# A two-layer SSM, attention and mixture-of-experts trunk: the layer loop written out, small loads moved to another queue, and v projected in two halves between scan steps

## The chip, the cores and the metric

The kernel runs on one core of one Trainium2 chip. The metric is the device time of one execution in microseconds (us), lower being better. A core has a matrix engine (TensorE, PE in the rows, with its weight loads as PEld), a vector engine (VectorE, DVE), an activation engine (ScalarE, ACT), a general engine (GpSimd, POOL) and a sync engine (SyncE, SP) that issues most of the transfers here. Each engine runs its own instructions in the order in which they are written; they meet through semaphores.

## What is computed

Everything is float32, with one sequence of 256 tokens of width 1024 and two layers. The reference, cut to what matters:

```python
for l in range(DEPTH):                                   # DEPTH = 2
    h = rms_norm(x, norm1_g[l])
    u, q, k, v, g_ssm, g_attn = jnp.split(h @ w_in[l], splits, axis=-1)
    y_ssm = s5_branch(u, a_re, a_im, log_dt, b_re, b_im, c_re, c_im, d_skip, w_glu)
    q = apply_rope(rms_norm(q, q_norm_g[l]), cos, sin)   # 8 heads of 64
    k = apply_rope(rms_norm(k, k_norm_g[l]), cos, sin)
    y_attn = moba_attention(q, k, v) @ w_attn[l]         # causal, 256 tokens
    x = x + (sigmoid(g_ssm) * y_ssm + sigmoid(g_attn) * y_attn) @ w_out[l]
    h2 = rms_norm(x, norm2_g[l])
    x = x + hier_moe(h2, ...)                            # 32 experts, 2 chosen per token

# s5_branch: dt = exp(log_dt); abar = exp((lam_re + i lam_im) dt); B scaled by f(abar, lam)
#   state[t] = abar * state[t-1] + B u[t];  y = Re(C state) + d * u;  z = gelu(y)
#   return (z @ w_glu)[:1024] * sigmoid((z @ w_glu)[1024:])
```

## The kernel before

Each of the five engines has one instruction stream, written out by hand, inside a hardware loop over the two layers (`Fori(0, DEPTH)`). A layer has a **front** (projections, state-space scan, attention, output projection, routing) and an **expert phase** of 11 units. A unit holds three experts (the last one two), and all 32 experts' weights are streamed through.

**Weights.** The tile `pool_all` is 11 slots of 2 MB (128 partitions by 4096 floats). SP issues every weight load, each when a semaphore says that the slot is free. In the front, slots 0 and 1 hold first the columns of u and q, then the gate columns of the state-space branch, then `w_glu`; slots 2 and 3 hold the columns of k and v, then the attention gates. `front_used` counts the uses that have ended. The same slots feed the expert units. Scratch of the front lives in the other slots.

**Small loads.** ACT's queue carries the rows for the gains and the poles (`rows`), the step sizes (`log_dt`), and B and C of the state-space model (`b_raw`, `c_raw`). Those of the first layer are issued at the start of the program. Those of the second layer are issued at the start of the first layer's expert phase. SP's queue carries the head gains (`qk_gain`) and the router's weights, behind the loads of slots 0 to 3.

**Order of the front.** PE: `project_u` (L586), `spread_rms` (L595), the three projections `project_qkv` of q, k and v (L610), `setup_matrices` (the transposes L555 and L562 of B and C), `scan_input` 0 and 1 (L628). Then come six steps of `gate(k)`, `scan_output(k)`, `scan_input(k + 2)` (L725, L643, L628), and then attention, mixed with gates 6 and 7, the last two `scan_output` and the GLU projection `ssm_project` (L757). DVE: `setup_first` (a serial chain of 128x16 and 128x32 operations, L1266 to L1351), the scaling of u, `angles` (L1249 to L1261), the head norms, `rope_k` for both halves (L1487 to L1494), `c_lhs` (L1542), and eight times `scan(k)` (L1416 to L1430) with `skip` (L1440) between. ACT: the sines, `heads_out` (L1064, L1068), the scaled copies of v (L1119), `b_lhs` (L1123), then `gate_tanh` (L1100) and `gelu` (L1077) in turn. POOL: `setup` (L1870 to L1882), the router's scaling (L1895), the rope tables (L1898, L1901), `rope_q` (L1961 to L1968), and eight times `rotate(k)` (L1918) with `gelu(k - 1)` (L1940 to L1950).

A scan step goes PE `scan_input`, DVE `scan`, POOL `rotate`, PE `scan_output`, DVE `skip`, POOL and ACT `gelu`. `setup_first` waits for the semaphore `setup_in`, which counts `log_dt` and all of B and C.

## Time and profile before

| | |
|---|---|
| median of 3 runs | 1474.98 us (1473.22 to 1476.66) |
| profiled execution, its own time | 1474.61 us |
| its span, first to last instruction | 1472.8 us |
| busy: PE, DVE, POOL, ACT | 1188.9, 434.6, 187.0, 159.7 us |
| moved by DMA | 462.28 MB, 314 GB/s over the span |

A timeline row gives the start in us, the duration, the engine (SPq and ACTq are transfers issued from those queues), the line in the kernel, the operation, output and input, and how many instructions were merged. Brackets at the end give how long the engine had been idle and what released it. "issue" there means that nothing in the profile was waited for. PE's float32 matmuls appear as two records each. The chain of waits runs back from the last instruction and shows at each step what was late.

### The profile page before, as it was taken

How to read it: one execution, taken by the hardware profiler on the slowest of the kernel's cores; microseconds unless marked ns; L12 is line 12 of the kernel's file. 1: busy time of each engine (PE TensorE's matmuls, PEld its weight loads, DVE VectorE, ACT ScalarE, POOL GpSimd, SP SyncE). 2: the span in 40 equal slices, each digit the busy share in tenths (PEclk: the TensorE clock that was granted, in tenths of full speed). 3: DMA queues.
4: the chain of work that ended last, by engine and by line, in shares of the span. 5: the costliest groups of instructions: out<-in, count | busy, mean ns of one | idle time of the engine just before them, and what ended most of it. 6: DMA issues, size and time to landing. Idle time of an engine off the chain costs nothing.

```text
span 1472.8 us, 19284 instructions
## 1 busy us (share of the span) xinstructions
PE 1188.9 (81%) x7371; PEld 541.1 (37%) x7372; DVE 434.6 (30%) x874; ACT 159.7 (11%) x313; POOL 187.0 (13%) x250
## 2 busy tenths in 40 slices
PE   7959799779777677777889888997778776778787
PEld 5334454524322233222254445444333232223232
DVE  1888622322101011101157894223111110011111
ACT  1230220300000000000013103112000000000000
POOL 0558600000000000000015574000000000000000
PEclk9969899899989899988999998998999988888889
DMA  9322067379999999999942220971999999999995
GB/s 296 136 93 115 1 254 321 123 329 428 428 429 428 429 429 429 429 428 428 422 165 114 115 115 16 383 285 51 427 428 429 428 429 429 429 428 428 429 429 227
DMA packets 57934, 462.28 MB, mean 314 GB/s; under 512 B 19964, under 2 KB 20120, under 8 KB 32280
## 3 DMA queue, kind: packets, MB, share of 16 engines
q1 hardware_dynamic: 46624, 460.39, 74.9%
q10 hardware_dynamic: 11256, 1.17, 0.7%
q8 instruction: 34, 0.56, 0.2%
q14 instruction: 20, 0.16, 0.0%
HBM read 460.49 MB, written 1.05 MB: 313 GB/s over the span
## 4 chain that ended last, share of the span: by engine, by line
DMA 40%; PE 36%; issue 7%; DVE 7%; POOL 6%; ACT 2%; SPq 1%; ACTq 1%; POOLq 0%; DVEq 0%
DMA pool_all<-in_w_gate_up_dram 39%; PE ps L912 15%; PE ps L757 4%; PE ps L781 4%; POOL pool_all L1918 3%; PE ps L929 2%; PE ps L725 2%; PE ps L739 2%; PE ps L873 2%; DVE pool_all L1430 1%; PE ps L586 1%; SPq L441 1%; PE ps L896 1%; PE ps L698 1%; ACTq L1016 1%
## 5 line engine op out<-in xcount | busy, mean ns | idle before, releaser
L912 PE MATMUL ps<-pool_all 128*32 128x512 f32 (+1 forms) x2816 | 368.8, 684 | 150.2 <-DMA pool_all<-in_w_gate_up_dram 150.2
L912 PEld LDWEIGHTS ps<-pool_all 128*32 128x32 f32 x2816 | 97.4, 124 | 416.7 <-issue 411.1
L929 PE MATMUL ps<-pool_all 128*32 128x512 f32 (+1 forms) x1408 | 160.6, 609 | 25.2 <-DMA pool_all<-in_w_down_dram 19.6
L1663 DVE SCALAR_TENSOR_TENSOR pool_all<-pool_all,ps 128x512 f32<-128x512 f32 x22 | 15.1, 688 | 547.6 <-ACT pool_all L1197 547.6
L725 PE MATMUL ps<-pool_all,hT 128*128 128x512 f32 x256 | 118.5, 617 | 0.0
L873 PE MATMUL ps<-pool_all,hT 128*128 128x128 f32 x704 | 92.1, 294 | 15.4 <-issue 10.7
L873 PEld LDWEIGHTS ps<-pool_all,hT 128*128 128x128 f32 x704 | 87.9, 207 | 32.4 <-issue 27.4
L929 PEld LDWEIGHTS ps<-pool_all 128*32 128x32 f32 x1408 | 45.9, 112 | 124.8 <-issue 124.7
L1197 ACT ACTIVATE pool_all<-ps 128x512 f32<-128x512 f32 x22 | 13.1, 597 | 688.7 <-PE ps L912 688.7
L1918 POOL TENSOR_TENSOR pool_all<-pool_all 128x512 f32<-128x512 f32 x64 | 79.7, 1279 | 40.0 <-DVE pool_all L1430 40.0
L610 PE MATMUL ps<-pool_all,hT 128*128 128x512 f32 x192 | 82.7, 592 | 0.0
L896 PE MATMUL ps<-pool_all 128*128 128x512 f32 x176 | 81.4, 605 | 0.0
L1870 POOL TENSOR_TENSOR pool_all<-pool_all,cst 128x512 f32<-128x512 f32 x4 | 4.2, 1065 | 575.0 <-DVE vec L1287 539.6
L725 PEld LDWEIGHTS ps<-pool_all,hT 128*128 128x128 f32 x256 | 49.2, 198 | 58.4 <-issue 57.3
L1676 DVE COPY pool_all<-ps 128x512 f32<-128x512 f32 x22 | 15.2, 692 | 177.3 <-PE ps L929 177.3
L757 PE MATMUL ps<-pool_all 128*128 128x512 f32 x128 | 56.5, 594 | 0.0
L781 PE MATMUL ps<-pool_all,hT 128*128 128x512 f32 x128 | 56.4, 594 | 0.0
L610 PEld LDWEIGHTS ps<-pool_all,hT 128*128 128x128 f32 x192 | 36.3, 190 | 45.0 <-issue 45.0
L896 PEld LDWEIGHTS ps<-pool_all 128*128 128x128 f32 x176 | 31.6, 189 | 50.0 <-issue 50.0
L643 PE MATMUL ps<-pool_all 128*32 128x128 f32 x512 | 19.9, 303 | 29.9 <-POOL pool_all L1918 29.8
L1653 DVE TENSOR_TENSOR pool_all<-ps,gain 128x512 f32<-128x512 f32 x44 | 30.0, 682 | 43.8 <-PE ps L873 43.8
L1416 DVE TENSOR_TENSOR pool_all<-ps,pool_all 128x512 f32<-128x512 f32 x64 | 39.6, 678 | 1.9 <-PE ps L628 1.7
(252 smaller groups left out, 982.5 us busy)
## 6 DMA issues: line engine op xcount, KB each, us to landing
pool_all<-in_w_gate_up_dram SPq DMA_DIRECT2D x128, 2048.0 KB, 25.4
pool_all<-in_w_down_dram SPq DMA_DIRECT2D x64, 2048.0 KB, 27.1
pool_all<-in_w_in_dram SPq DMA_DIRECT2D x16, 2048.0 KB, 12.6
pool_all<-in_w_glu_dram SPq DMA_DIRECT2D x4, 2048.0 KB, 11.0
pool_all<-in_w_out_dram SPq DMA_DIRECT2D x4, 2048.0 KB, 20.0
pool_all<-in_w_attn_dram SPq DMA_DIRECT2D x2, 2048.0 KB, 7.4
xs<-in_x_dram SPq DMA_DIRECT2D x1, 1024.0 KB, 5.1
out_dram<-xs SPq DMA_DIRECT2D x2, 512.0 KB, 2.8
```

What stands on the lines that cost most here:

```text
L610: mm = pe.matmul(ps[:, bank + t], hT[:, k, t * P:(t + 1) * P], wide_slot(slot + k // 4)[:, k % 4, col:col + 512], start=(k == 0), stop=(k ...
L725: mm = pe.matmul(ps[:, GATE_BANK[j]], hT[:, k, t * P:(t + 1) * P], wide_slot(slot + k // 4)[:, k % 4, 512 * half:512 * half + 512], start= ...
L739: mm = pe.matmul(ps[:, u % 2], oT[:, c, t * P:(t + 1) * P], wide_slot(2)[:, c, 512 * half:512 * half + 512], start=(c == 0), stop=(c == 3))
L757: mm = pe.matmul(ps[:, GLU_BANK[u] + w], uT[:, k, t * P:(t + 1) * P], slot_cols(k // 2).rearrange("p (k c n) -> p k c n", k=2, c=2)[:, k % ...
L781: mm = pe.matmul(ps[:, WO_BANK[t] + half], hT[:, k, t * P:(t + 1) * P], wide_slot(9 + k // 4)[:, k % 4, 512 * half:512 * half + 512], star ...
L873: mm = pe.matmul(ps[:, 2 + k // 4, (k % 4) * P:(k % 4 + 1) * P], x_rows[:, t, k], pick[:, t], start=(t == 0), stop=(t == NT - 1))
L896: mm = pe.matmul(ps[:, 4 + 2 * t + half], backT[:, t], ybuf[:, half], start=first, stop=False, skip_group_check=True)
L912: mm = pe.matmul(ps[r, half], xT[:, k, r], lane_cols(n, TRIO * h, k % 4, half), start=(k == 0), stop=(k == KC - 1), skip_group_check=True)
L929: mm = pe.matmul(ps[r, 2 + half], ffT[:, c, r], lane_cols(n, 2 * TRIO, c, half), start=(c == 0), stop=(c == 3), skip_group_check=True)
L1416: ve.tensor_tensor(out4[o], x, table, ALU.mult).then_inc(dve_layer, 1)
L1653: ve.tensor_tensor(xT[:, 4 * h:4 * h + 4], ps[:, 2 + h].rearrange("p (k s) -> p k s", k=4), wide(gain2[:, 4 * h:4 * h + 4], 2, [4, P]), AL ...
L1918: pool.tensor_tensor(post[:, v], wst[:, r], table[:, tiles, 0:HALF], ALU.mult).then_inc(rotated, 1)
```

## The change

1. **The layer loop is written out** on all five engines: `for l in range(DEPTH)` in Python. The hardware branches at the layer boundary are gone, and so are the last layer's preparations for a layer that doesn't exist. The loops over expert units stay.
2. **Small loads.** `log_dt` joins the rows on ACT's queue, and its semaphore is now `rows_in`. B, C and the head gains go on SP's queue, between slots 0 and 1 and slots 2 and 3, under `setup_in`. DVE's `setup_first` waits for `rows_in` alone.
3. **v** is no longer projected before the scan. `project_v(0)` and `project_v(1)`, one 128-token tile each, take the places of `gate(0)` and `gate(1)` in the steps, and every gate moves two steps down. The steps are eight now, and attention begins after the eighth.
4. **DVE's `rope_k`** moves from ahead of the scan to between `skip(6)` and `skip(7)`.
5. **POOL's scaling of the router's weights** moves from ahead of the rope tables to the end of its layer.

The diff, cut to its core:

```diff
-        with sp.Fori(0, DEPTH) as l:
+        for l in range(DEPTH):
...
             load_rows(0, win_d, 0, U0)
             load_rows(1, win_d, 4, U0)
-            sp.wait_ge(unit_used, at(unit_used, l, -1))
+            for r, b in enumerate((ssm_b_re, ssm_b_im)):
+                load_setup(b_raw[:, r], b[one_layer].rearrange("o (i g) s h -> (o g s) i h", g=2))
+            for r, c in enumerate((ssm_c_re, ssm_c_im)):
+                load_setup(c_raw[:, r], c[one_layer].rearrange("o (q g) h s -> (o g h) q s", q=QUADS))
+            for w, g in enumerate((q_norm_g, k_norm_g)):
+                load_setup(qk_gain[:, w], g[one_layer].to_broadcast([P, HD]))
+            if l:
+                sp.wait_ge(unit_used, at(unit_used, l, -1))
             load_rows(2, win_d, 0, V0)
...
+            def project_v(t):
+
+                pe.wait_ge(b_ready, at(b_ready, l, 4))
+                for k in range(KC):
+                    mm = pe.matmul(ps[:, t], hT[:, k, t * P:(t + 1) * P], wide_slot(2 + k // 4)[:, k % 4, 512:1024],
+                                   start=(k == 0), stop=(k == KC - 1))
+                mm.then_inc(front_used if t else v_mm, 1)
...
-            project_qkv("q")
-            project_qkv("k")
-            project_qkv("v")
+            project_qk("q")
+            project_qk("k")
             setup_matrices(l)
             scan_input(0)
             scan_input(1)
-            for k in range(6):
-                gate(k)
+            for k in range(8):
+                if k < NT:
+                    project_v(k)
+                else:
+                    gate(k - NT)
                 scan_output(k)
-                scan_input(k + 2)
+                if k < 6:
+                    scan_input(k + 2)
             turn_heads(0)
-            scan_output(6)
+            gate(6)
             turn_heads(1)
             scores(0)
-            gate(6)
+            gate(7)
             turn_probs(0)
             scores(1)
-            scan_output(7)
             values(0)
-            gate(7)
+            ssm_project(0)
             turn_probs(1)
...
-            ve.wait_ge(setup_in, at(setup_in, n, per[setup_in.name]))
+            ve.wait_ge(rows_in, at(rows_in, n, per[rows_in.name]))
...
             skip(6)
+            rope_k(0)
+            rope_k(1)
+            skip(7)
             softmax_in(0)
-            skip(7)
             attention_out(0)
```

How instructions stand now. PE after the projections of q and k, before: three groups L610 (q, k, v), the two groups of transposes, `scan_input` 0 and 1 (L628), `gate(0)` (L725).

```order
L595 MATMUL ps<-pool_all,cst 128x128 x2
L610 MATMUL ps<-pool_all,hT 128x512 x16
L576 ISA
L610 MATMUL ps<-pool_all,hT 128x512 x16
L603 REGISTER_ALU
L610 MATMUL ps<-pool_all,hT 128x512 x16
L550 ISA
L552 REGISTER_ALU
L555 MATMUL ps<-cst,pool_all 128x128 x8
L562 MATMUL ps<-cst,pool_all 128x128 x8
L628 MATMUL ps<-pool_all 128x128 x16
```

The same place after: L616 is q and k together, L624 is a half of v, L640 is `scan_input`, L655 is `scan_output`.

```order
L604 MATMUL ps<-pool_all,cst 128x128 x2
L616 MATMUL ps<-pool_all,hT 128x512 x32
L564 MATMUL ps<-cst,pool_all 128x128 x8
L571 MATMUL ps<-cst,pool_all 128x128 x8
L640 MATMUL ps<-pool_all 128x128 x16
L624 MATMUL ps<-pool_all,hT 128x512 x8
L655 MATMUL ps<-pool_all 32x128 x16
L640 MATMUL ps<-pool_all 128x128 x8
L624 MATMUL ps<-pool_all,hT 128x512 x8
```

The 16 matmuls of v have left the stretch ahead of the first scan step and stand as two groups of 8 in the first two steps.

PE at the end of the scan, before: `gate(5)`, `scan_output(5)`, `scan_input(7)`, the turn of q (L658), `scan_output(6)`, the turn of k, `scores(0)` (L680), `gate(6)`.

```order
L725 MATMUL ps<-pool_all,hT 128x512 x8
L640 REGISTER_ALU
L643 MATMUL ps<-pool_all 32x128 x16
L628 MATMUL ps<-pool_all 128x128 x8
L658 MATMUL ps<-cst,pool_all 128x128 x8
L640 REGISTER_ALU
L643 MATMUL ps<-pool_all 32x128 x16
L658 MATMUL ps<-cst,pool_all 128x128 x8
L680 MATMUL ps<-pool_all 128x128 x8
L725 MATMUL ps<-pool_all,hT 128x512 x8
```

After, from `gate(4)` (L737) on; L670 is a turn and L692 is `scores(0)`.

```order
L737 MATMUL ps<-pool_all,hT 128x512 x8
L655 MATMUL ps<-pool_all 32x128 x16
L737 MATMUL ps<-pool_all,hT 128x512 x8
L655 MATMUL ps<-pool_all 32x128 x16
L670 MATMUL ps<-cst,pool_all 128x128 x8
L737 MATMUL ps<-pool_all,hT 128x512 x8
L670 MATMUL ps<-cst,pool_all 128x128 x8
L692 MATMUL ps<-pool_all 128x128 x8
L737 MATMUL ps<-pool_all,hT 128x512 x8
```

Both turns and `scores(0)` now stand behind the last `scan_output`.

SP at the start of a layer, after (before, the two small loads of the head gains stood behind all four loads of `w_in`, and B and C were not on this queue):

```order
L431 DMA pool_all<-in_w_in_dram 128x4x1024 x2
L444 DMA pool_all<-in_ssm_b_re_dram 128x16x16
L444 DMA pool_all<-in_ssm_b_im_dram 128x16x16
L444 DMA pool_all<-in_ssm_c_re_dram 128x4x64
L444 DMA pool_all<-in_ssm_c_im_dram 128x4x64
L444 DMA qk_gain<-in_q_norm_g_dram 128x64
L444 DMA qk_gain<-in_k_norm_g_dram 128x64
L431 DMA pool_all<-in_w_in_dram 128x4x1024 x2
L438 DMA router_w<-in_router_w_group_dram 128x8x4
```

The weights of k and v (the second L431) now stand behind six small loads.

## Rows read from the trace of the kernel before

**Rows 1.** The chain that ended last, by line, from the page.

```profile
DMA pool_all<-in_w_gate_up_dram 39%; PE ps L912 15%; PE ps L757 4%; PE ps L781 4%; POOL pool_all L1918 3%; PE ps L929 2%; PE ps L725 2%; PE ps L739 2%; PE ps L873 2%; DVE pool_all L1430 1%; PE ps L586 1%; SPq L441 1%; PE ps L896 1%; PE ps L698 1%; ACTq L1016 1%
```

**Rows 2.** Timeline, first layer: DVE's setup chain, first angle, ACT's first head output.

```profile
35.58 0.18 DVE L1266 TENSOR_SCALAR pool_all<-log_dt 128x32 f32<-128x32 f32 x1 [22.03 <-DMA pool_all<-in_ssm_c_im_dram]
...
50.41 1.67 DVE L1249 TENSOR_TENSOR pool_all<-cst,turns_hi 128x1032 f32<-128x1032 f32 x1
...
72.65 1.25 ACT L1064 ACTIVATE pool_all<-ps,rstd 128x512 f32<-128x512 f32 x2
```

**Rows 3.** Timeline, first layer, PE: project_u, and q with k and v behind it.

```profile
12.54 15.83 PE L586 MATMUL ps<-hT,pool_all 128*128 128x256 f32 x64 [0.88 <-DMA pool_all<-in_w_in_dram]
...
28.65 31.92 PE L610 MATMUL ps<-pool_all,hT 128*128 128x512 f32 x74
```

**Rows 4.** First layer: last rows load, PE's turn; log_dt's two loads, to landing.

```profile
2.48 0.55 ACTq L1005 DMA_DIRECT2D rows<-in_ssm_a_im_dram  x1
...
7.74 0.32 PE L545 MATMUL ps<-cst,rows 52*128 52x52 f32 x1 [7.74 <-DMA rows<-in_ssm_a_im_dram]
...
DMA to landing us min/median/max: 3.1/5.3/7.4
```

**Rows 5.** B's first load for layer two; a window (columns: busy, PEclk, DMA, GB/s).

```profile
288.51 0.40 ACTq L1016 DMA_DIRECT2D pool_all<-in_ssm_b_re_dram  x1
...
296.00:300.00 4.00, 4.00 (x42) 1.17 (x36) 2.82 (x15) 0.00 (x0) 0.00 (x0) 1.00 0.00 0
```

**Rows 6.** Timeline, first layer, from the head norms to the first scan steps.

```profile
80.48 1.25 ACT L1119 ACTIVATE pool_all<-ps,rstd 128x512 f32<-128x512 f32 x2
...
80.99 0.69 DVE L1487 TENSOR_TENSOR pool_all<-pool_all,head_ss 128x512 f32<-128x512 f32 x1
...
84.18 3.77 PE L628 MATMUL ps<-pool_all 64*128 64x128 f32 x32 [3.12 <-ACT pool_all L1123]
...
93.24 2.48 DVE L1416 TENSOR_TENSOR pool_all<-ps,pool_all 128x512 f32<-128x512 f32 x4
...
95.63 0.68 DVE L1419 TENSOR_TENSOR pool_all<-pool_all 128x512 f32<-128x512 f32 x1
...
99.66 5.03 POOL L1918 TENSOR_TENSOR pool_all<-pool_all 128x512 f32<-128x512 f32 x4 [10.33 <-DVE pool_all L1430]
...
102.09 1.56 DVE L1419 TENSOR_TENSOR pool_all<-pool_all 128x512 f32<-128x512 f32 x1
```

**Rows 7.** Timeline at the layers' boundary and in the second layer's front.

```profile
752.75 16.07 PE L586 MATMUL ps<-hT,pool_all 128*128 128x256 f32 x64 [5.47 <-issue]
...
754.96 0.08 DVE L1378 MEMSET ov_slot<- 128x28 f32 x1 [4.22 <-issue]
...
766.99 0.17 DVE L1351 TENSOR_TENSOR f_im<-f_im,den 128x16 f32<-128x16 f32 x1
...
770.90 1.77 DVE L1249 TENSOR_TENSOR pool_all<-cst,turns_hi 128x1032 f32<-128x1032 f32 x1
...
792.13 1.25 ACT L1064 ACTIVATE pool_all<-ps,rstd 128x512 f32<-128x512 f32 x2
...
822.25 5.03 POOL L1918 TENSOR_TENSOR pool_all<-pool_all 128x512 f32<-128x512 f32 x4 [13.88 <-DVE pool_all L1430]
```

**Rows 8.** Timeline, first layer, from the end of the scan to ssm_project(2).

```profile
158.77 1.06 PE L658 MATMUL ps<-cst,pool_all 128*128 128x128 f32 x8 [0.69 <-ACT pool_all L1100]
...
169.57 4.58 POOL L1918 TENSOR_TENSOR pool_all<-pool_all 128x512 f32<-128x512 f32 x4 [1.11 <-DVE pool_all L1430]
...
171.74 2.08 PE L680 MATMUL ps<-pool_all 64*128 64x128 f32 x16 [1.25 <-ACT pool_all L1134]
...
173.75 8.51 PE L725 MATMUL ps<-pool_all,hT 128*128 128x512 f32 x16
...
186.97 7.09 PE L725 MATMUL ps<-pool_all,hT 128*128 128x512 f32 x16
...
216.68 7.03 PE L757 MATMUL ps<-pool_all 128*128 128x512 f32 x16
```

More of the change, by code:

```diff
@@ L571, in _ @@
         norm(0)
-        with pe.Fori(0, DEPTH) as l:
+        for l in range(DEPTH):
             def weights(i, turn):
@@ L834, in _ @@
             values(1)
-            ssm_project(0)
+            ssm_project(1)
             turn_probs(2)
             values(2)
-            ssm_project(1)
             turn_attention()
@@ L919, in unit @@
                     pe.wait_ge(main["xT"], at(main["xT"], l, 2 * i + 4))
-                if last:
+                if last and l < DEPTH - 1:
                     setup_vectors(l + 1)
@@ L994, in _ @@
             unit(UNITS - 1, 2, duo_lanes, last=True)
-            pe.nop()
-            with pe.If(l < DEPTH - 1):
+            if l < DEPTH - 1:
                 norm(l + 1)
-            pe.nop()
     @block.scalar
@@ L1047, in _ @@
         norm_squares(0)
-        load_setup(0)
-        with act.Fori(0, DEPTH) as l:
+        for l in range(DEPTH):
             act.dma_start(gain2, norm2_g[bass.ds(l, 1)].rearrange("o (p k) -> (o p) k", k=KC)).then_inc(gain_in, 16)
@@ L1116, in _ @@
             heads_std(1)
-            act.wait_ge(front_used, at(front_used, l, 2))
-            for t in range(NT):
-                act.activation(vtok[:, t], ps[:, 6 + t], ACT.Copy, scale=rstd[:, t:t + 1]).then_inc(v_raw, 1)
             act.wait_ge(bt_mm, at(bt_mm, l, 1))
@@ L1124, in _ @@
                                    scale=const("odd_tile")[:, o:o + 1]).then_inc(b_ready, 1)
-            for k in range(6):
-                gate_tanh(k)
+            for k in range(8):
+                if k < NT:
+                    if k == 0:
+                        act.wait_ge(v_mm, at(v_mm, l, 1))
+                    else:
+                        act.wait_ge(front_used, at(front_used, l, 2))
+                    act.activation(vtok[:, k], ps[:, k], ACT.Copy, scale=rstd[:, k:k + 1]).then_inc(v_raw, 1)
+                else:
+                    gate_tanh(k - NT)
                 gelu(k)
@@ L1131, in _ @@
                 act.copy(qT[:, 2 * n:2 * n + 2].rearrange("p c s -> p (c s)"), ps[:, n]).then_inc(qT_ready, 1)
+            gate_tanh(6)
             act.wait_ge(qk_turned, at(qk_turned, l, 2))
@@ L1135, in _ @@
             exps(0)
-            gelu(6)
-            gate_tanh(6)
+            gate_tanh(7)
             probs_turned(0)
             exps(1)
-            gelu(7)
-            gate_tanh(7)
+            glu_sigmoid(0)
             probs_turned(1)
             exps(2)
-            glu_sigmoid(0)
+            glu_sigmoid(1)
             probs_turned(2)
-            glu_sigmoid(1)
             act.wait_ge(o_turned, at(o_turned, l, 1))
@@ L1373, in _ @@
         norm_scale(0)
-        with ve.Fori(0, DEPTH) as l:
+        for l in range(DEPTH):
             L = counted(dve_layer, l)
```

71 lines of the change are left out of this document (26 added, 45 removed).

## The prediction

> **What bounds the kernel now.** I read the chain of waits first. 39% of the span in it is the experts' gate and up weights arriving, and the lines of PE, DVE and POOL that follow belong to the two fronts [rows 1]. So the kernel alternates: from the second expert unit of each layer on it runs at the pace of its weight stream, which this change leaves alone in bytes and order, and before that a front runs in which compute engines hand work to each other. Every load of the first expert units is tied to a step of the front, so a front that ends earlier by some time moves the expert phase by the same time. The question is what the change does to each front.
>
> Then I read the timeline of the first front for what is late. Three stretches matter.
>
> Stretch one is up to the first head output. DVE sits idle 22.03 us until 35.58, waiting for C's last load, and only then starts its serial chain. The angles start at 50.41 and ACT's first head output, T below, at 72.65, which is 22.2 us after the angles [rows 2]. PE is far ahead: `project_u` runs from 12.54 to 28.4 and q, k and v follow without a gap, at 74 records in 31.92 us, so 13.8 us for each projection of 32 records [rows 3].
>
> Stretch two is from T to the first `rotate`. It holds ACT's copies of v (80.48), DVE's `rope_k` from 80.99, PE's `scan_input` at 84.18, DVE's first scan at 93.24 and POOL's first `rotate` at 99.66, before which POOL was idle 10.33 us [rows 6]. DVE decides it, as PE's operands for the scan were there 9 us before DVE came.
>
> Stretch three is the scan and what follows. From the first `rotate` at 99.66 to the last, which ends at 174.15, POOL and DVE set the pace, and from `scores(0)` at 171.74 PE has hardly an idle moment up to `ssm_project(2)` at 216.68 [rows 6, 8].
>
> In the second layer DVE doesn't wait for loads. There PE idles 5.47 us and DVE 4.22 us for nothing that the profile shows, exactly at the branch that closes the layer loop. u runs from 752.75 to 768.8, the angles start at 770.90, T is 792.13 and the first `rotate` is at 822.25 [rows 7].
>
> **Stretch one, first layer.** DVE now waits for the rows and `log_dt` only. Its chain then lies beside `project_u`: in the second layer it takes 12.2 us from the first memset to its last product (754.96 to 767.16) [rows 7]. Started at about 14.5 it ends near 27, ahead of u. The next to be late is PE's u. In the second layer the angles start 2.1 us after u ends (768.8 to 770.90) [rows 7], so with u's end at 28.4 they would start at 30.5. One cost comes in: PE's turn of the rows waits for all loads under `rows_in`, now with `log_dt`, and PE's 3.9 us of work between the turn (7.74) and its readiness for u (12.54 less the 0.88 of waiting) stands behind it. ACT issues `log_dt` after the last rows load, so from 3.0, and its two loads took 3.1 and 7.4 us to land [rows 3, 4]. Landing at 6.1 costs nothing, landing at 10.4 makes u start at 14.3, 1.8 us late. I take 1.3, near the loaded case. The angles then start at 31.8, 18.6 us earlier than 50.41, and T is 54.0. The projection of k ends near 57.5 (u's end 29.7, two times 13.8, and the small spread between them), and ACT needs it 3.9 us after T, so it just fits.
>
> B, C and the head gains now travel ahead of the weights of k. Alone, the B and C loads had all landed within 7.5 us of the first issue (288.51 to 296.00) [rows 5]. Before, all that was issued at the start had landed by 35.6 [rows 2], the bytes are the same, and PE needs the k columns at 43.7 (u's end and one projection). So this costs 0, and if it is late, each us late is a us of k. POOL's setup hides behind q and k.
>
> **Stretch one, second layer.** Without the branch PE goes on from the turn of x at 747.3, so u ends by about 763. DVE's memsets follow its norm at 750.8 instead of 754.96, so its chain ends at 763.0, a little later than u, and the angles start at 764.6, which is 6.3 us earlier. T is 785.8. If the gap stays, the gain here is 0.
>
> **Stretch two.** `rope_k` and the v copies have gone. From T, ACT's b operands took until PE's 84.18, which is 11.5 us, and lose the 1.1 us of the two v copies: 10.4. DVE's scan starts when the first of the two scan inputs is in, for which I take 1.6, a little under half of their 3.77 us, at T + 12.0, since its own `c_lhs` is done by then. The scan took 6.4 us (93.24 to 99.6). But it now runs beside POOL's `rope_q`, which ended at 99.66 less 10.33, so at 89.33 or T + 16.7. The DVE addition L1419 took 0.68 us with POOL idle and 1.56 us beside `rotate` [rows 6], and the scan has two such operations there, so I add 1.9 (0 to 2.6). The first `rotate` starts at T + 20.3. First layer: 54.0 + 20.3 = 74.3 against 99.66, a gain of **25.3**. Second layer: 785.8 + 20.3 = 806.1 against 822.25, a gain of **16.1**.
>
> The Trainium skill (SBUF — State Buffer, section "SBUF: two separate sides") says that a DVE operation with two SBUF inputs and a GpSimd operation take one pair of ports by an exclusive lock, and that the other blocks wholly. It speaks against moving the scan beside `rope_q`, and the two L1419 rows agree with it; without it this stretch would be 1.9 us shorter in each layer.
>
> **Stretch three.** The eight scan steps keep their order on DVE and POOL. v's halves are as long as the gates they replace. Steps seven and eight now hold `gate(4)` and `gate(5)` where PE was half idle. What is paid is the attention: two turns and `scores(0)` stood in those idle times and now stand behind the last `scan_output`. Counted from the end of the last `rotate`, against before:
> - ACT frees the banks for the turn only after `gelu(6)` and `gate_tanh(5)`: +2.5, in which `scan_output(7)` hides, -1.1
> - two turns at 1.06: +2.1; k's copy to SBUF between turn and scores, as ACT's pair of v copies (1.25): +1.2
> - `scores(0)`: 2.08 at the low clock, about half at the high one: +1.6
> - `gate(6)` was 8.51 us on a PE that had idled, `gate(7)` 7.09: -1.4; it had begun 0.4 before the `rotate` ended: +0.4
> - the last `rotate` beside `rope_k` instead of an idle DVE, 5.03 against 4.58 us: +0.45
> - `turn_attention` follows `values(2)` at once and waits for DVE: +0.9
>
> That is **6.7 us** lost in each layer [rows 6, 8]. The bounds are 4 (the turns find idle PE time after all) and 10 (`rope_k`, which filled most of 80.99 to 93.24 before the scan, holds up `skip(7)` and with it ACT, whose copies of q stand behind `gelu(7)`). What follows `ssm_project(2)` is in the same order.
>
> **Sum.** First layer 25.3 - 6.7 = 18.6. Second layer 16.1 - 6.7 = 9.4. The last layer's dropped turn of rows is 0.3. Together 28.3 us off the profiled execution's 1474.61: 1446.3. The median of the runs shown is 0.4 above that execution, so I predict **1446.7**.
>
> **Rivals.**
> 1. *The boundary gap stays.* For it: the profile names no releaser, and expert loops are left just before, with a branch of their own. Against it: both gaps sit at the loop's end. Then the second layer's 6.3 is lost: 1453.0. Chance 0.12. The Trainium skill (Runtime: NRT & Kernel Launch, section "Instruction fetch mechanics") says that a taken branch out of the prefetched window stalls the engine for a fetch, and recommends unrolling. By it the gap goes, and I lean that way.
> 2. *The small loads hold the weights of k.* PE found slot 1 landed in the middle of u, at 20.5. If B and C then take the 22 us that DVE waited for them beside the weights [rows 2], and the 4.2 MB behind them 13.4 at the mean 314 GB/s of the table, slots 2 and 3 land at 55.9 instead of by 43.7, and the first layer pays 12.2: 1458.9. Chance 0.06.
> 3. *Slower.* The same mechanism in both layers, with the k columns late by more than 28 us in all: the head gain is eaten and the 6.7 of stretch three remains twice. With both head gains gone it gives 1474.98 + 13.4 = 1488.4. It decides from slots 2 and 3 landing some 19 us late in the first layer and 10 in the second. The 7.5 us of rows 5 speak against it. Chance 0.04.
> 4. *The costs are smaller.* `log_dt` lands early (1.3), no contention (3.8), and waits on constants instead of registers save a little: 1441. Chance 0.12.
> 5. The forecast, 1443 to 1451 with its own bounds: 0.66.
>
> **Range.** Low: the cheap case with the tail's lower bound, 1439. High: the forecast with the gap kept and 2 us more of tail in each layer, 1457. About 0.2% is what a measurement of this kernel can tell from no change; rival 3 and a strong form of rival 2 are all that reaches it. Faster 0.94, same 0.02, slower 0.04.
>
> **What would show it.** In the changed profile: DVE's chain starts before 16 us; u starts at 12.5 to 14.4 with the turn of the rows waiting for `log_dt`; PE never waits for `w_in` in k; POOL's first `rotate` is near 74 us; no idle of 4 us on PE or DVE at the boundary, and the second layer's `rotate` comes some 59 us after the turn of x; `ssm_project(2)` starts 124 us after the first `rotate`, where it was 117. I am wrong if the first `rotate` is later than 80, if k waits for its weights, or if the tail is over 130.

## The result and the profile after

The changed kernel takes 1448.93 us (median of 4 runs, 1448.35 to 1455.68) against 1474.16 for the kernel before timed beside it, a ratio of 0.9837 with a 95% interval of 0.9805 to 0.9869. The profiled execution took 1449.39 us, span 1447.5, where that of before had 1474.61 and 1472.8. Timed once more later, on a chip beside two experiments, it took 1451.35 (1448.58 to 1454.80), ratio 0.9838 (0.9821 to 0.9854). Its eight runs spread over 7 us, so a difference of 2 or 3 us from it says little.

The forecast was 1446.7, so the time came out as predicted, 2 us on the slow side. The inside of the sum did not come out as well, and the experiments below found several terms that stand on other reasons than the ones the prediction gave.

The chain of waits by line, from the page of the changed kernel, answers [rows 1]. The experts' weights still head it:

```profile
DMA pool_all<-in_w_gate_up_dram 40%; PE ps L925 15%; POOL pool_all L1912 6%; PE ps L769 4%; PE ps L793 4%; DVE pool_all L1427 4%; PE ps L942 2%; PE ps L737 2%; PE ps L751 2%; PE ps L886 2%; SPq L441 1%; PE ps L909 1%; PE ps L710 1%; DMA log_dt<-in_ssm_log_dt_dram 1%; PE ps L815 0%
```

First front, timeline of the changed kernel (start, length, engine, line, operation; in brackets the idle time before and what ended it). PE's turn of the rows and `project_u`, the start of DVE's chain, the first angle, ACT's first head output T:

```profile
11.30 0.32 PE L554 MATMUL ps<-cst,rows 52*128 52x52 f32 x1 [11.30 <-DMA log_dt<-in_ssm_log_dt_dram]
...
14.84 13.98 PE L595 MATMUL ps<-hT,pool_all 128*128 128x256 f32 x64
...
17.07 0.18 DVE L1263 TENSOR_SCALAR pool_all<-log_dt 128x32 f32<-128x32 f32 x1
...
52.95 1.25 ACT L1064 ACTIVATE pool_all<-ps,rstd 128x512 f32<-128x512 f32 x2
```

DVE's 22.03 us of idle time [rows 2] are gone and T came 19.7 us earlier. Stretch two, from T to the first `rotate`:

```profile
63.40 3.78 PE L640 MATMUL ps<-pool_all 64*128 64x128 f32 x32 [2.84 <-ACT pool_all L1120]
...
65.51 2.48 DVE L1413 TENSOR_TENSOR pool_all<-ps,pool_all 128x512 f32<-128x512 f32 x4 [2.55 <-PE ps L640]
67.91 0.90 DVE L1416 TENSOR_TENSOR pool_all<-pool_all 128x512 f32<-128x512 f32 x1
68.73 0.68 DVE L1418 TENSOR_TENSOR pool_all<-pool_all 128x512 f32<-128x512 f32 x1
...
72.22 5.05 POOL L1912 TENSOR_TENSOR pool_all<-pool_all 128x512 f32<-128x512 f32 x4 [3.96 <-DVE pool_all L1427]
```

It takes 19.3 us (72.22 less 52.95) where it took 27.0, and ends with the first `rotate` at 72.22 instead of 99.66 [rows 6]. PE after the scan, which answers [rows 8]:

```profile
148.04 1.08 PE L655 MATMUL ps<-pool_all 128*32 128x128 f32 x32 [1.84 <-POOL pool_all L1912]
151.05 1.83 PE L670 MATMUL ps<-cst,pool_all 128*128 128x128 f32 x8 [1.93 <-ACT pool_all L1100]
152.67 7.99 PE L737 MATMUL ps<-pool_all,hT 128*128 128x512 f32 x16
...
162.79 1.16 PE L692 MATMUL ps<-pool_all 64*128 64x128 f32 x16 [1.25 <-ACT pool_all L1139]
...
198.63 7.03 PE L769 MATMUL ps<-pool_all 128*128 128x512 f32 x16
```

`ssm_project(2)` (L769) starts 126.4 us after the first `rotate`, 9.4 more than before. At the layer boundary (PE and ACT of the second layer, against [rows 7]):

```profile
727.25 2.04 PE L546 MATMUL ps<-cst,xs 128*128 128x128 f32 x16
729.13 13.98 PE L595 MATMUL ps<-hT,pool_all 128*128 128x256 f32 x64
...
769.33 1.25 ACT L1064 ACTIVATE pool_all<-ps,rstd 128x512 f32<-128x512 f32 x2
```

PE's 5.47 us of idle time have gone. The first `rotate` of this layer is at 788.61, before 822.25.

A table that serves for all experiments, from the same rows of each trace: "end of u" is the end of `project_u`, R the first `rotate`, A the start of the matmul that numbers the assigned tokens, the first one behind the router. T to R is stretch two; R to A holds the scan, the attention and the projections behind them.

| profiled kernel | layer 0: T | T to R | R | R to A | layer 1: end of u | T | T to R | R to A | span |
|---|---|---|---|---|---|---|---|---|---|
| before | 72.65 | 27.0 | 99.66 | 185.6 | 768.82 | 792.13 | 30.1 | 186.1 | 1472.8 |
| changed | 52.95 | 19.3 | 72.22 | 195.2 | 743.11 | 769.33 | 19.3 | 195.0 | 1447.5 |
| e1 loops only | 72.54 | 27.1 | 99.68 | 185.4 | 760.69 | 785.78 | 28.0 | 184.8 | 1462.1 |
| e2 without part three | 53.42 | 29.3 | 82.69 | 186.1 | 744.69 | 771.09 | 27.2 | 184.8 | 1446.6 |
| e3 log_dt apart | 53.61 | 19.3 | 72.89 | 195.2 | 743.50 | 769.86 | 19.3 | 194.9 | 1447.9 |
| e4 turn of q early | 53.42 | 19.3 | 72.72 | 192.3 | 740.64 | 766.99 | 19.3 | 192.0 | 1442.1 |
| e5 k's rotary ahead | 52.70 | 27.1 | 79.84 | 193.4 | 748.69 | 774.98 | 27.1 | 191.5 | 1457.1 |
| e6 v in the gap | 52.62 | 19.3 | 71.91 | 184.8 | 732.77 | 759.21 | 19.5 | 184.6 | 1427.4 |
| e7 B, C on ScalarE's queue | 65.17 | 19.3 | 84.44 | 195.2 | 755.30 | 780.06 | 19.3 | 199.1 | 1463.0 |
| e8 the same, behind the sines | 53.24 | 19.3 | 72.51 | 198.1 | 746.95 | 771.69 | 19.3 | 194.6 | 1449.0 |
| e9 part three alone | 72.57 | 19.0 | 91.60 | 197.8 | 773.84 | 797.02 | 19.8 | 194.7 | 1475.4 |
| e10 changed, again | 53.63 | 19.3 | 72.92 | 196.3 | 745.20 | 771.20 | 19.3 | 198.0 | 1453.0 |

### The profile page after: what moved, and what is told of

Read it like the earlier page. It is cut to its first block, busy times and chain, and to the rows that moved or that the text cites. A ratio compares the mean times of both kernels' runs of the same rounds, so it can differ in the third digit from the quotient of the medians.

```text
span 1447.5 us, 18361 instructions
## 1 busy us (share of the span) xinstructions
PE 1182.6 (82%) x7370; PEld 536.1 (37%) x7371; DVE 436.0 (30%) x873; ACT 159.8 (11%) x313; POOL 190.2 (13%) x250
## 4 chain that ended last, share of the span: by engine, by line
DMA 40%; PE 35%; DVE 11%; POOL 7%; issue 3%; ACT 3%; SPq 1%; ACTq 0%; DVEq 0%; POOLq 0%
DMA pool_all<-in_w_gate_up_dram 40%; PE ps L925 15%; POOL pool_all L1912 6%; PE ps L769 4%; PE ps L793 4%; DVE pool_all L1427 4%; PE ps L942 2%; PE ps L737 2%; PE ps L751 2%; PE ps L886 2%; SPq L441 1%; PE ps L909 1%; PE ps L710 1%; DMA log_dt<-in_ssm_log_dt_dram 1%; PE ps L815 0%
## 5 line engine op out<-in xcount | busy, mean ns | idle before, releaser
L942 PE MATMUL ps<-pool_all 128*32 128x512 f32 (+1 forms) x1408 | 159.7, 606 | 22.4 <-DMA pool_all<-in_w_down_dram 15.0
L737 PE MATMUL ps<-pool_all,hT 128*128 128x512 f32 x256 | 116.3, 608 | 0.0
L886 PEld LDWEIGHTS ps<-pool_all,hT 128*128 128x128 f32 x704 | 89.2, 209 | 30.2 <-issue 30.0
L737 PEld LDWEIGHTS ps<-pool_all,hT 128*128 128x128 f32 x256 | 48.5, 195 | 56.8 <-issue 55.4
L769 PE MATMUL ps<-pool_all 128*128 128x512 f32 x128 | 56.5, 594 | 0.0
L793 PE MATMUL ps<-pool_all,hT 128*128 128x512 f32 x128 | 56.4, 593 | 0.0
L616 PE MATMUL ps<-pool_all,hT 128*128 128x512 f32 x128 | 55.3, 592 | 0.0
L909 PEld LDWEIGHTS ps<-pool_all 128*128 128x128 f32 x176 | 31.6, 189 | 50.0 <-issue 50.0
L616 PEld LDWEIGHTS ps<-pool_all,hT 128*128 128x128 f32 x128 | 24.2, 190 | 29.7 <-issue 29.7
L769 PEld LDWEIGHTS ps<-pool_all 128*128 128x128 f32 x128 | 23.9, 190 | 27.7 <-issue 27.7
## 6 DMA issues: line engine op xcount, KB each, us to landing
pool_all<-in_w_in_dram SPq DMA_DIRECT2D x16, 2048.0 KB, 12.2
pool_all<-in_w_out_dram SPq DMA_DIRECT2D x4, 2048.0 KB, 18.6
```

The costliest lines, as they stand in the source:

```text
L616: mm = pe.matmul(ps[:, bank + t], hT[:, k, t * P:(t + 1) * P], wide_slot(slot + k // 4)[:, k % 4, col:col + 512], start=(k == 0), stop=(k ...
L737: mm = pe.matmul(ps[:, GATE_BANK[j]], hT[:, k, t * P:(t + 1) * P], wide_slot(slot + k // 4)[:, k % 4, 512 * half:512 * half + 512], start= ...
L769: mm = pe.matmul(ps[:, GLU_BANK[u] + w], uT[:, k, t * P:(t + 1) * P], slot_cols(k // 2).rearrange("p (k c n) -> p k c n", k=2, c=2)[:, k % ...
L793: mm = pe.matmul(ps[:, WO_BANK[t] + half], hT[:, k, t * P:(t + 1) * P], wide_slot(9 + k // 4)[:, k % 4, 512 * half:512 * half + 512], star ...
L886: mm = pe.matmul(ps[:, 2 + k // 4, (k % 4) * P:(k % 4 + 1) * P], x_rows[:, t, k], pick[:, t], start=(t == 0), stop=(t == NT - 1))
L909: mm = pe.matmul(ps[:, 4 + 2 * t + half], backT[:, t], ybuf[:, half], start=first, stop=False, skip_group_check=True)
```

## The experiments

The change has three parts: the loops written out, the small loads moved, and v with k's rotary moved. e1 and e2 cut the change at its joints.

**e1, the loops alone.** On every engine, and the conditions inside the loop (`If` on l) written out with it, so that loop branch and `If` are tested together:

```
-        with pe.Fori(0, DEPTH) as l:
+        for l in range(DEPTH):
```

> The kernel before with its five hardware layer loops written out and nothing else (small loads, v and k's rotary as before). If the gap at the layer boundary (PE idle 5.47 us and VectorE idle 4.22 us, both 'issue') belongs to the loop's branch, it goes, in the second layer alone: about 5.5 us less than the kernel before, 1468.7 (1467 to 1470), and PE's u projection follows the turns of x with no idle time of its own. If the gap is that of instructions fetched for the first time, it stays: 1474 plus or minus 1. Layer 0 is the same to 0.3 us in both theories.

Measured: 1464.45 us (1463.94 to 1465.59), ratio 0.9928 (0.9912 to 0.9945), some 10.5 us less and not 5.5. Layer 0 is unchanged (A at 285.09, before 285.26), so all of it is behind the boundary. PE there:

```profile
744.83 2.04 PE L537 MATMUL ps<-cst,xs 128*128 128x128 f32 x16
746.71 13.98 PE L586 MATMUL ps<-hT,pool_all 128*128 128x256 f32 x64
```

The idle time has gone, as predicted, and `project_u` fell from 16.07 to 13.98 us as well. The granted clock says why. The window 752.75 to 757.50 of the kernel before, and the like one of e1 (columns: length, busy PE, PEld, DVE, ACT, POOL, then PEclk, DMA share, GB/s):

```profile
752.75:757.50 4.75, 4.75 (x13) 3.87 (x14) 1.99 (x13) 0.00 (x0) 0.00 (x0) 0.57 0.06 11
```

```profile
744.80:751.50 6.70, 6.70 (x40) 5.95 (x39) 5.49 (x21) 5.05 (x7) 0.00 (x0) 1.00 1.03 400
```

After 5.47 us of idle time PE worked at a granted 0.57, so mostly at the lower of its two levels (1.2 GHz), where e1 has 1.00. A gap of 5.5 us on PE costs PE 7.7 (turn of x to end of u: 23.58 before, 15.86 in e1). In e1 v is still ahead of the scan and bounds it, so R comes 8.1 us sooner behind the turn of x (68.96 against 77.01). R to A gives 1.3 more, and the remaining 1.3 lie behind A, in the expert phases.

**e2, the change without its third part.** `project_qkv("v")` stands behind k again, `rope_k` ahead of the scan, gates and tail are in the order of before:

```
-            project_qk("q")
-            project_qk("k")
+            project_qkv("q")
+            project_qkv("k")
+            project_qkv("v")
             setup_matrices(l)
```

> The changed kernel with its third part undone: v projected whole behind k, both v copies ahead of the b copies, k's rotary ahead of the scan, gates and tail in the order of before; loops written out and small loads on the weight queue stay. Theory P: the table T is ready at 53 us in layer 0 again, but now v's projection (14.3 us) stands between k (done 56.7) and the turns of b, so they run at 71, and rotate(0) at 86 to 87, some 14 us later than in the changed kernel; the tail gives 9.4 back; so 4.9 us are lost in layer 0 and 2.0 in layer 1 (T to rotate(0) 30.1 and tail 117.5 as before, against 19.3 and 126.4): 1455.8 us (1453 to 1458). Theory R: v is no bound, T to rotate(0) is 27.0 as in the kernel before, rotate(0) at 80; then the third part is worth next to nothing in either layer: 1449 (1447 to 1451).

Measured: 1448.22 us (1447.44 to 1449.15), ratio 0.9816 (0.9799 to 0.9832). That is as fast as the changed kernel, or a little faster. Theory P has the mechanism: in e2 PE's q, k and v run from 29.87 for 41.37 us and the turn of B follows at once:

```profile
71.07 1.04 PE L564 MATMUL ps<-cst,pool_all 128*128 128x128 f32 x8
...
75.00 2.06 PE L637 MATMUL ps<-pool_all 64*128 64x128 f32 x32 [2.01 <-ACT pool_all L1119]
```

But R is at 82.69 and not at 86 to 87: behind v it takes 11.6 us from the turn of B to R, and behind k, where ACT's head norm must first be done, 15.7. So part three brings R forward by 10.5 us in layer 0, and in layer 1 T to R by 7.9, and pays 9.1 and 10.2 for it from R to A. Net: nothing. Theory R's number was right and its reason wrong. Point 5 of the change (POOL's scaling of the router's weights) is still in e2 and so is counted with the small loads; it was not tested alone. Its operation takes 1.11 us, and POOL was idle 9.26 us ahead of `rope_q` in the kernel before, so I expect nothing of it.

**e9, part three alone**, on the kernel before:

> The kernel before with the third part of the change alone: v in two halves between the scan steps, k's rotary in the tail, the tail's order of the changed kernel; hardware loops and small loads as before. Theory 1 (the tail takes back what v gives): T to rotate(0) falls from 27.0 and 30.1 to 19.3 us, rotate(0) to ssm_project(2) rises from 117.0 and 117.5 to 126.4, so +1.7 us in layer 0 and -1.9 in layer 1: 1475 us (1473 to 1477). Theory 2: the part's worth depends on the other two, and alone it loses: 1478 or more.

Measured: 1477.4 us (1473.7 to 1480.4, 10 runs), ratio 1.0019 (1.0009 to 1.0030). A loss of 3 us, at the border of both theories. T to R is 19.0 and 19.8 as Theory 1 has it, and R to A 197.8 and 194.7, so the tail takes back all and 2 to 3 us more. That more is seen in many kernels with part three; it is taken up under e10.

**e5, k's rotary ahead of the scan**, v left in halves:

```
+            rope_k(0)
+            rope_k(1)
             ve.wait_ge(ct_mm, at(ct_mm, l, 1))
...
             skip(6)
-            rope_k(0)
-            rope_k(1)
             skip(7)
```

> The changed kernel with k's rotary (rope_k of both tiles, on VectorE) back ahead of the scan, v's halves left between the scan steps. Theory 1: VectorE ends last in the second stretch, and rope_k, some 10 us beside GpSimd's rope_q, goes straight onto it: T to rotate(0) 27 us instead of 19.3, and the tail gives back only what rope_k costs there, the slower last rotate (5.67 against 5.04) and about 1 us of waits: rotate(0) to ssm_project(2) 125 instead of 126.4. So 6.3 us lost per layer: 1461.5 us (1459 to 1464). Theory 2: the tail is long because VectorE turns k there while TensorE waits; without it the tail falls to 120 or less and the move is worth nothing: 1449 to 1452.

Measured: 1458.63 us (1457.6 to 1459.2), ratio 0.9888 (0.9872 to 0.9905), 9.7 more than the changed kernel and a little under Theory 1's range of 1459 to 1464. Theory 1 in kind: T to R 27.1 in both layers, against 27 expected. The tail gave back 1.8 and 3.5 us, a little more than the 1.4 expected. DVE's `rope_k` and POOL's second `rope_q` side by side:

```profile
61.84 1.64 DVE L1486 TENSOR_TENSOR pool_all<-pool_all,rope 128x512 f32<-128x512 f32 x1
...
68.36 1.64 DVE L1486 TENSOR_TENSOR pool_all<-pool_all,rope 128x512 f32<-128x512 f32 x1
70.03 0.88 DVE L1489 TENSOR_TENSOR pool_all<-pool_all,rope 128x256 f32<-128x256 f32 x2
```

The pair of `rope_k` takes 10.5 us here (61.11 to 71.6), and POOL's pair of `rope_q` 12.2 instead of 10.8. So part three is two things of opposite sign: k's rotary out of stretch two is worth about 5 us a layer (e5 against the changed kernel; 3.6 against its second timing, 1451.35), and v's move with its order of the tail costs about as much (e5 against e2, which differ by that alone: 10.4 us in two layers).

**e3, log_dt on its own semaphore.**

```
-            ve.wait_ge(rows_in, at(rows_in, n, per[rows_in.name]))
+            ve.wait_ge(dt_in, at(dt_in, n, 16))
```

> The changed kernel with log_dt on a semaphore of its own, so that TensorE's turn of the 52 rows waits for the other five loads only and VectorE's exponential waits for log_dt. Theory 1: the 2.3 us by which u starts later than before (14.84 against 12.54) come back in full in layer 0: 1446.6. Theory 2: u's projection is held by its weights' landing, so it starts at 12.5 and takes 15.8 us again instead of 14.0, ends at 28.4 as in the kernel before, and the saving is 0.3 to 0.5 us: 1448.5. Nothing changes in layer 1.

Measured: 1450.75 us (1449.76 to 1451.31), ratio 0.9834 (0.9818 to 0.9851). No gain, as Theory 2 has it, but only half by its picture:

```profile
7.96 0.32 PE L554 MATMUL ps<-cst,rows 52*128 52x52 f32 x1 [7.96 <-DMA rows<-in_ssm_a_im_dram]
...
14.12 15.74 PE L595 MATMUL ps<-hT,pool_all 128*128 128x256 f32 x64 [2.27 <-DMA pool_all<-in_w_in_dram]
```

PE is ready 3 us earlier and waits 2.27 us for `w_in`. So the landing of `w_in` sets u's start, at 14.12, only 0.7 us before the changed kernel's 14.84. Yet u ends at 29.86, 1.0 later. Its 15.74 us hold no wait: they hold the low clock. Two windows of e3 inside u (columns: length, busy PE, PEclk, DMA share, GB/s), and the first records of u in the kernel before:

```profile
16.00:18.00 2.00, 2.00 (x7) 0.50 1.04 411
20.00:22.00 2.00, 2.00 (x11) 1.00 1.14 154
```

```profile
L586 PE MATMUL ps<-hT,pool_all x8: 594/631/792, 12.5 to 15.7; 128*128 128x256 f32 x8
```

In e3 a record of u takes 634 ns at a granted 0.50 and 379 ns at 1.00. In the kernel before the first eight take some 631 ns, up to about 16.1 us, and the rest 379; in the changed kernel's first profile all 64 take 379 to 382. In its second profile the first five take some 634, and u ends at 30.1 instead of 28.8. So what u takes in layer 0, 13.98 to 15.83 us, is nearly all TensorE's clock at the start of the program, and it differs between two executions of one program.

**e7, B and C back on ScalarE's queue.** log_dt stays with the rows, and DVE waits only for these:

```
         norm_squares(0)
+        load_setup(0)
```

> The changed kernel with the loads of B and C back on ScalarE's queue as in the kernel before, log_dt staying with the rows and VectorE's setup waiting only for these. It asks which half of part two brought T forward by 19.7 us. Theory 1: that VectorE no longer waits for B and C is all of it: B and C land at about 35.6 us, GpSimd's setup starts at 35.7 instead of 28.2 and ends by 57, T stays at 53, rotate(0) is at most 1 us later: 1449 to 1451 us. Theory 2: GpSimd's later setup ends last (the turn of B waits for it, or rope_q for its tables), and rotate(0) of layer 0 moves by 5 to 7 us: 1454 to 1456.

Measured: 1464.7 us (1464.4 to 1465.0), ratio 0.9931 (0.9914 to 0.9947). Both theories missed: the loss is 15.8 us, and it is not where either put it. T itself is 12.2 us late. The other 3.6 stand beside a low clock: layer 1's R to A is 4.1 us longer, and from 920 to 936 us, around waits of 1.16 and 0.73 us, the granted clock is 0.79 where the changed kernel has 1.00 (more under e10). e7's four runs lie within 0.6 us, so for e7 this need not be chance; what ties it to the loads, if anything, is not shown. ACT and its queue in e7, and DVE's wait:

```profile
8.44 8.27 ACTq L1044 DMA_DIRECT2D pool_all<-in_ssm_b_im_dram  x1
...
16.74 17.79 ACTq L1044 DMA_DIRECT2D pool_all<-in_ssm_c_re_dram  x1
34.56 0.55 ACTq L1044 DMA_DIRECT2D pool_all<-in_ssm_c_im_dram  x1
...
35.71 1.28 ACT L1032 ACT_TABLE_LOAD   x1 [26.13 <-issue]
37.00 0.21 ACT L1032 ACTIVATE pool_all<-pool_all 128x16 f32<-128x16 f32 x1
```

```profile
37.43 0.17 DVE L1333 TENSOR_TENSOR pool_all<-pool_all 128x16 f32<-128x16 f32 x1 [11.55 <-ACT pool_all L1033]
```

ACT did nothing else while it issued these loads: two issues of 8.27 and 17.79 us, 26.13 us idle. Behind them stood a sine over 16 columns that DVE's chain needs. In the kernel before the same issues stood there (c_re took 9.50 us, to 31.60), hidden behind DVE's own wait for C. The Trainium skill (Perfetto Trace Analysis, section What "DMA-bound" means) counts the sequencer of the issuing engine among the things that can bound a kernel, when its track is solid with DMA slices; by that rule ACT's track from 8.0 to 35.1 is the row to look at, and the trace agrees.

**e8, the same with ACT's two small sines ahead of the loads**, a test of that reading:

```
             setup_one(l)
+            if l == 0:
+                load_setup(0)
             for h in range(2):
```

> The kernel of the run before (B and C loaded through ScalarE's queue) with one change of order in layer 0: ScalarE computes its two small sines of the setup first (they can run at 22.1 us) and issues the four loads of B and C behind them. In the run before, ScalarE stood in the issue of those loads from 8.0 to 35.1 us, and VectorE waited for the small sines until 37. Theory 1: that held engine is the 12 us that were lost, T comes back to 53 or 54 us in layer 0, B and C land between 30 and 38 us, GpSimd's setup still ends before 60: 1449 to 1453 us. Theory 2: it is the landing of B and C that matters, later still here, and T or the turn of B stays where it was or comes later: 1462 to 1468.

Measured: 1452.23 us (1450.85 to 1454.85), ratio 0.9856 (0.9840 to 0.9872). Theory 1: T is back at 53.24, and R at 72.51 is where the changed kernel has it.

```profile
21.36 0.22 ACT L1032 ACTIVATE pool_all<-pool_all 128x16 f32<-128x16 f32 x1 [10.46 <-DVE pool_all L1321]
...
21.79 7.25 ACTq L1044 DMA_DIRECT2D pool_all<-in_ssm_b_im_dram  x1
29.06 5.04 ACTq L1044 DMA_DIRECT2D pool_all<-in_ssm_c_re_dram  x1
...
53.24 1.25 ACT L1072 ACTIVATE pool_all<-ps,rstd 128x512 f32<-128x512 f32 x2
```

C's last load lands at about 37 us, in the changed kernel at 23.0, and POOL's setup starts at 37.48 instead of 28.22 (there it waits for the head gains under the same semaphore). This costs nothing at R. So of the 19.7 us that part two took off T, in the order in which the runs take the causes away, 7.5 are DVE's wait for B and C (72.65 to e7's 65.17) and 12.2 are ACT's freedom from issuing them. Two things limit this split. By estimate, with issues no longer than in the kernel before, where ACT was through at 33.3 us and not at 35.7, it would be some 9.9 and 9.8. And the two hide each other. No run has DVE wait with ACT free; POOL, which waits for that semaphore in the changed kernel, starts 11.2 us after DVE's chain, so by estimate DVE's wait alone would still cost some 11. Both had to go. That B and C land early is worth nothing as soon as neither DVE nor ACT stands behind them.

**e4, the turn of q ahead of the last scan output.**

```
+                if k == 7:
+                    turn_heads(0)
                 scan_output(k)
...
-            turn_heads(0)
             gate(6)
```

and on ACT `gate_tanh(5)` ahead of `gelu(6)`.

> The changed kernel with ScalarE's tanh of gate(5) put ahead of its gelu(6), and TensorE's turn of q put ahead of scan_output(7). In the changed kernel the turn of q stands at 151.05 us behind two idle times of TensorE (1.84 and 1.93 us) and takes 1.83 us, gate(6) 7.99 us, both longer than the 1.04 and 7.13 they take elsewhere. Theory 1: those waits and the slow start are what the tail costs beyond the 6.7 us of the prediction: the turn runs at 146.9, gate(6) at about 149.1 with 7.1 us, scores(0) at 158.4 instead of 162.8, so 4.4 us less in each layer: 1440.1 us (1438.5 to 1442). Theory 2: the next wait (k's rotary, done at 152.4; ScalarE's copies behind gelu(7)) takes over, and under 2 us per layer are saved: 1445 to 1448.

Measured: 1443.8 us (1443.6 to 1445.4), ratio 0.9789 (0.9772 to 0.9805), 5.1 less than the changed kernel (7.6 less than its second timing) and not 8.8. Up to `scores(0)` it went as Theory 1 says:

```profile
147.63 1.07 PE L670 MATMUL ps<-cst,pool_all 128*128 128x128 f32 x8 [0.87 <-ACT pool_all L1101]
148.63 1.08 PE L655 MATMUL ps<-pool_all 128*32 128x128 f32 x32
149.64 7.13 PE L737 MATMUL ps<-pool_all,hT 128*128 128x512 f32 x16
...
158.90 1.16 PE L692 MATMUL ps<-pool_all 64*128 64x128 f32 x16 [1.25 <-ACT pool_all L1142]
```

R to the first `ssm_project` fell by 4.4 us (102.7 to 98.3). Then 1.5 of it was lost again, not to a wait but to the clock: the turn of the attention took 1.97 us instead of 1.09 and the `ssm_project` behind it 7.70 instead of 7.03.

**e6, v's first half in PE's gap.** Part of v goes ahead of `scan_input(0)`, into bank 7, and all gates move up one step:

```
+            project_v(0, range(0, 3))
             scan_input(0)
+            project_v(0, range(3, KC))
             scan_input(1)
             for k in range(8):
-                if k < NT:
-                    project_v(k)
+                if k == 0:
+                    project_v(1)
                 else:
-                    gate(k - NT)
+                    gate(k - 1)
+                if k == 7:
+                    turn_heads(0)
```

Behind the scan, `gate(7)` is split around the turn of k, and `ssm_project(0)` to `(3)` fill the waits of the attention batches.

> The changed kernel with TensorE's gates one scan step earlier: v's first half into the free bank 7, three eighths of it in the idle time ahead of scan_input(0) and the rest between scan_input(0) and scan_input(1), its second half in step 0, gate(k) in step k+1, the turn of q and ScalarE's tanh of gate(5) and copies of q ahead of the last gelu, and the four parts of ssm_project used as filler of the attention batches. Theory 1: the tail's length is TensorE's work, pushed out behind the scan by v; with one gate (7.1 us) less behind the scan and the waits of 1.8, 1.9 and 1.3 us filled, T to rotate(0) stays at 19.3 to 20.3 and the end of attention comes 8 to 11 us earlier in each layer: 1430 us (1425 to 1436). Theory 2: something beside TensorE's work bounds the tail (softmax on VectorE and ScalarE between scores and the turns of the probabilities, or a weight's landing), and it stays near the kernel with the early turn of q: 1440 (1438 to 1444).

Measured: 1429.19 us (1427.8 to 1429.6), ratio 0.9688 (0.9672 to 0.9704). This beats both kernels: 19.7 us less than the changed one and 46 less than before. T to R stays (19.3 and 19.5) and R to A is 184.8 and 184.6, about 10.4 less in each layer, Theory 1's 8 to 11. PE in the gap and behind the scan:

```profile
60.13 2.74 PE L625 MATMUL ps<-pool_all,hT 128*128 128x512 f32 x6
63.13 1.16 PE L644 MATMUL ps<-pool_all 64*128 64x128 f32 x16 [0.26 <-ACT pool_all L1130]
64.22 4.56 PE L625 MATMUL ps<-pool_all,hT 128*128 128x512 f32 x10
69.56 1.16 PE L644 MATMUL ps<-pool_all 64*128 64x128 f32 x16 [0.78 <-ACT pool_all L1140]
```

```profile
150.00:185.00 35.00, 34.80 (x147) 19.27 (x146) 14.47 (x24) 12.21 (x42) 3.33 (x8) 1.00 0.60 241
```

From 150 to 185 PE is busy 34.80 of 35 us at a granted 1.00.

**e10, the changed kernel again.**

> The changed kernel itself, timed beside the two others on this chip, to set part three's worth against the run without it (1448.2): 1448 to 1450 us if the worth is nothing, 1446 or less if it is a gain of two or more.

Measured: 1451.35 us (1448.58 to 1454.80). So part three (e2's 1448.22) is worth nothing, or costs up to 3 us. Its profiled execution took 1454.80, that of the same program above 1449.39, and the two traces show what spreads these times. PE of layer 1 at `values(2)` and the turn of the attention, in e10 and then in the earlier profile:

```profile
913.35 2.22 PE L710 MATMUL ps<-pool_all 128*128 128x64 f32 x16 [1.16 <-ACT pool_all L1092]
916.30 1.97 PE L718 MATMUL ps<-cst,pool_all 128*128 128x128 f32 x8 [0.73 <-DVE pool_all L1471]
```

```profile
911.36 2.00 PE L710 MATMUL ps<-pool_all 128*128 128x64 f32 x16 [1.16 <-ACT pool_all L1092]
914.09 1.09 PE L718 MATMUL ps<-cst,pool_all 128*128 128x128 f32 x8 [0.73 <-DVE pool_all L1471]
```

The waits are the same, 1.16 and 0.73 us. In e10 the granted clock falls there and is 0.93 on average from 918 to 947 us, in the other profile it is 1.00 from 916 to 945, and R to A is 198.0 against 195.0. Across all profiles with part three's tail this happens in some layers and not in others (194.6 to 199.1 where neither the turn of q is early nor k's rotary ahead of the scan); the kernels with the tail of before stay within 184.8 to 186.1.

## Why the prediction came out, and where it did not

**Stretch one, first layer: right in time, half right in cause.** T was put at 54.0 and came at 52.95. Two terms were off and mostly cancelled: log_dt landed 8.2 us after its issue (3.10 to 11.30), beyond the 7.4 that had served as the bad case, so u started at 14.84, above the 14.4 given; and u took 13.98 us, not 15.8. The prediction had read 15.83 us as u's own length, and the 16.07 of layer 1 seemed to confirm it; but both held a stretch at the low clock (e1, e3), and the work at the high clock is 13.98. That the high clock was there from the start of u was luck: in the changed kernel's second profile it wasn't, and T was 53.63. What log_dt's lateness costs is not settled to better than 1 us. e3 takes it away and gains nothing, but its own u ran 1.8 us longer at the low clock. What the step missed is ACT: it counted DVE's wait for C as the whole of the 18.6 us. e7 and e8 show that with this wait gone and ACT still issuing only 7.5 of 19.7 come, and that the rest came with moving the issue off ACT. The forecast held because the change did both.

**Small loads ahead of k's weights: right, by a margin of some 4.5 us.** k never waited (L616 is one run of 27.63 us from 29.10), and rival 2 fell. But the long issue did not vanish: it went to SP, in front of k's weights.

```profile
4.03 15.00 SPq L444 DMA_DIRECT2D pool_all<-in_ssm_b_im_dram  x1
...
21.96 0.98 SPq L431 DMA_DIRECT2D pool_all<-in_w_in_dram  x2
```

The later of k's two slots took 16.0 us to land from its issue at 22.4, so it was in at 38.4, and PE came to k at about 42.9 (half of the 27.63 us). e8 adds that the early landing of B and C was not needed.

**Stretch one, second layer: right that the gap goes, its price too small and then not all spent.** The boundary was priced at 6.3 us. PE gains 7.7 there (e1: 5.6 of gap, 2.1 of low clock), but in the changed kernel DVE's chain is next to be late: it ends at 745.9, 13.2 us after its first memset at 732.7 instead of the 12.2 taken (11.7 in e1), because POOL's setup now runs beside its start. The angles come 20.2 us after the turn of x begins, before 25.7: 5.5 gained, of which 4.8 are left at T, as the way from the angles to T took 21.9 us instead of 21.2. By the rule of the Trainium skill (Runtime: NRT & Kernel Launch, section "Instruction fetch mechanics") that the prediction leaned on, the trace agrees: written-out loops have no such gap. That the gap was a fetch is not shown by any row. Rival 1 fell.

**Stretch two: right but for two terms.** The forecast was T + 20.3, measured 19.3 in both layers, and within 0.5 us of it in every kernel of the table that has part three whole. The 1.9 us for DVE beside POOL's `rope_q` were wrong: `rope_q` ended at T + 15.3 and not at T + 16.7, since DVE, idle 2.55 us before its scan, no longer slowed it, and only one addition was touched (0.90 against 0.68). Against this the scan began at T + 12.6, not 12.0: PE's first scan input took 2.1 us and not 1.6. With `rope_k` beside it (e5) both are slow. The rule of the Trainium skill named there (SBUF — State Buffer, section "SBUF: two separate sides") holds for the rows of e5; whether the two engines would meet at all was the point to work out. First `rotate`: 72.22, predicted 74.3; in layer 1 59.3 us after the turn of x ended (729.29), predicted some 59.

**Stretch three: the wrong size, 9.4 in place of 6.7.** Of the 2.7 us more, 0.7 arose before the last `rotate` ended: it ends 75.7 us after the start of the first, before 74.5, and 0.45 of that was in the list (it took 5.67 us beside `rope_k`, not 5.03). 2.0 lie behind it, and 1.7 of them are PE behind the wait of 1.93 us: the turn of q took 1.83 and not 1.06, and `gate(6)` 7.99 and not 7.09, at a granted 0.82 from 147.9 to 153. The list took the high clock for granted at the very place where it put a new wait. This is the term that was mis-sized. In layer 1 the tail cost 8.9. The bound of 10 held.

**The sum.** Layer 0 gave 18.05 us at `ssm_project(2)` (216.68 less 198.63; predicted 18.6), layer 1 another 6.7 at the same place (predicted 9.4), and the end 0.5 more: 25.3 of span against 28.3. The tail missed by 4.9 over both layers and layer 1's stretch one by 1.5; stretch two (2.0 for both) and layer 0's stretch one (1.1) gave part of it back.

**What the prediction did not ask** is what each part is worth alone. It gave v's part a gain of 6.7 to 9.8 in stretch two against a loss of 6.7, so near zero in layer 0 and 3.1 in layer 1. By e1, e2 and e10 the loops are worth 10 to 11 us, the small loads 16, and part three nothing; by e9, on the kernel before, part three costs 3.

Not settled is why the granted clock falls at the same two short waits in one run and not in another. And e6 changed three things at once (v's place, the early turn of q, the filling of the attention's waits); e4 gives 5.1 us for the second, the other two were not parted.

## What to carry to other kernels

Before a load is moved, look at the issuing engine as well as at the waiting one: the time of the issue row was time in which ACT did nothing else, and a tiny operation behind it carried the whole front. The long issue goes along with the load, so look also at what stands behind it in the new place (15.00 us on SP here, in front of k's weights). Moving work out from ahead of a serial loop gains only if the loop's slack can hold it; count the engine's busy time per step first (here 9.37 us of PE work in steps of 9.4 to 10.9 us), else the same work comes out at the far end. And a gap removed from TensorE was worth its length plus the slow start behind it (5.6 and 2.1 us in e1), as an added wait cost both (1.93 and 1.7 us in the changed kernel's tail).
